# Attention's product with V by tiles of 128 queries, and GpSimd's first row requests placed behind the first mixed low parts

## The reference, cut to what matters

```
for i in range(2):
    y = rms_norm(h, mix_norm[i]);  proj = y @ w_in[i]
    mixed = concatenate([lru_out * silu(g_lru), ret_out * silu(g_ret), sgu_out * silu(g_sgu)])   # 2048 wide
    h = h + mixed @ w_out[i]
    z = rms_norm(h, ple_norm[i]);  h = h + sigmoid(z @ w_ple_gate[i]) * (p[i] @ w_ple_proj[i])
```

```
mod = silu(cond) @ w_ada + b_ada                       # shifts, scales and gates, 6 x 1024
s = einsum('bqkgd,bskd->bkgqs', q, k) * 128 ** -0.5    # 4 query heads, 2 key heads, 512 queries, 768 keys
o = einsum('bkgqs,bskd->bqkgd', softmax(s), v)
x = x + gt1 * (concatenate([o, conv], -1) @ w_out)
x = x + gt2 * moe_ffn(modulate(x, ...))                # 32 experts, 4 per token
```

## Time and profile before

| | |
|---|---|
| time, median of 3 runs | 2527.57 us (2526.86 to 2530.43) |
| the profiled execution's own time | 2525.92 us |
| its span | 2524.1 us |
| PE busy | 2420.9 us, 96% of the span |
| DVE, ACT, POOL busy | 2036.4, 1319.5, 683.3 us |
| mean granted TensorE clock | 0.977 of full speed |

### The profile page before, as it was taken

How to read it: one execution, slowest core, us unless ns; L and a number is a source line. 1 busy time by engine, 2 the same in 40 slices (tenths; PEclk the granted TensorE clock), 3 DMA queues, 4 the chain that set the end, 5 groups by cost and what they waited for, 6 DMA issues and landing times.

```text
span 2524.1 us, 31372 instructions
## 1 busy us (share of the span) xinstructions
PE 2420.9 (96%) x10771; PEld 1934.3 (77%) x10771; DVE 2036.4 (81%) x1844; ACT 1319.5 (52%) x1206; POOL 683.3 (27%) x407
## 2 busy tenths in 40 slices
PE   8999999999999999998869999999999999999995
PEld 7777778786877787874657888888888888888884
DVE  7788587576885786884259999999999999999994
ACT  4442223334323244334327777777777777777772
POOL 5333341342423432340221222122112211221120
PEclk9999999999999999999969999999999999999998
DMA  6232245222422652220049999999999999999992
GB/s 236 83 130 71 75 152 174 67 76 78 139 67 82 257 211 69 75 93 1 13 177 372 367 373 366 378 365 372 368 371 370 373 361 380 361 372 368 375 358 96
DMA packets 104426, 572.47 MB, mean 227 GB/s; under 512 B 14192, under 2 KB 14336, under 8 KB 54288
## 3 DMA queue, kind: packets, MB, share of 16 engines
q1 hardware_dynamic: 86784, 515.15, 53.9%
q0 software_dynamic: 17280, 56.20, 7.7%
q10 hardware_dynamic: 288, 0.14, 0.0%
HBM read 559.37 MB, written 24.12 MB: 231 GB/s over the span
## 4 chain that ended last, share of the span: by engine, by line
PE 89%; DVE 6%; ACT 2%; issue 1%; DVEq 1%; DMA 1%; ACTq 0%; SPq 0%; POOLq 0%
PE ps L1479 85%; PE ps L1157 2%; DVE scr L2180 1%; DVE y_split L2117 1%; PE ps L665 0%; DVE mix L2231 0%; DVE scr L2229 0%; DMA mix<-acc_rows 0%; DVE scr L948 0%; DVEq L2127 0%; PE ps L701 0%; DMA acc_rows<-rows,lst 0%; DVE w_split L1284 0%; PE ps L1409 0%; DVE hT L2377 0%
## 5 line engine op out<-in xcount | busy, mean ns | idle before, releaser
L1284 DVE TENSOR_TENSOR w_split<-raw,w_split 128x2048 fp32r<-128x2048 f32 x386 | 877.3, 2287 | 54.6 <-ACT w_split L1236 43.5
L1479 PE MATMUL ps<-y_split,pieces_split 128*128 128x512 f32 x3600 | 846.9, 396 | 19.6 <-POOLq L2547 7.8
L1236 ACT ACTIVATE w_split<-raw 128x2048 fp32r<-128x2048 f32 x386 | 736.1, 1916 | 197.8 <-PE ps L1479 178.2
L1479 PEld LDWEIGHTS ps<-y_split,pieces_split 128*128 128x128 f32 x3600 | 681.9, 190 | 172.4 <-issue 29.0
L1479 PE MATMUL ps<-w_split,rows_T 128*128 128x512 f32 x3096 | 752.2, 394 | 1.9 <-DVE rows_T L1290 1.9
L1479 PEld LDWEIGHTS ps<-w_split,rows_T 128*128 128x128 f32 x3096 | 575.5, 188 | 119.4 <-DVE rows_T L1290 2.5
L2535 POOL TENSOR_TENSOR pieces_split<-pieces,pieces_split 128x1024 fp32r<-128x1024 f32 x151 | 373.2, 2482 | 653.5 <-ACT pieces_split L1813 524.9
L1813 ACT ACTIVATE pieces_split<-pieces 128x1024 fp32r<-128x1024 f32 x144 | 151.3, 1058 | 434.5 <-PE ps L1479 403.2
L1479 PE MATMUL ps<-w_split,hidden_T 128*128 128x512 f32 x1536 | 363.7, 392 | 1.7 <-DVE hidden_T L1290 1.7
L1479 PEld LDWEIGHTS ps<-w_split,hidden_T 128*128 128x128 f32 x1536 | 285.8, 188 | 72.5 <-DVE hidden_T L1290 13.5
L1348 POOL COPY rows_i<-slot_tokens 128x1 int32 (+1 forms) x34 | 59.5, 1750 | 407.7 <-PE ps L1157 374.0
(11 more groups left out here) (265 smaller groups left out, 2074.9 us busy)
## 6 DMA issues: line engine op xcount, KB each, us to landing
raw<-in_w_moe SPq DMA_DIRECT2D x386, 1024.0 KB, 7.5
pieces<-in_pieces SPq DMA_DIRECT2D x181, 512.0 KB, 3.6
scr<-in_ada POOLq DMA_DIRECT2D x48, 512.0 KB, 5.4
scr<-in_ple SPq DMA_DIRECT2D x2, 1536.0 KB, 7.0
acc_rows<-in_zeros POOLq DMA_DIRECT2D x5, 512.0 KB, 10.9
hT<-in_xT SPq DMA_DIRECT2D x8, 256.0 KB, 5.5
h_rows<-scr SPq DMA_DIRECT2D x4, 512.0 KB, 3.5
mix<-acc_rows SPq DMA_DIRECT2D x4, 512.0 KB, 5.1
```

The lines of the kernel that those rows point to most:

```text
L1236: nc.scalar.activation(wsp[:, p % SPLIT, 0], raw[:, p % RAW, :], ACT.Copy).then_inc(high, 3 if p == 1 else 1)
L1284: nc.vector.tensor_tensor(wsp[:, p % SPLIT, 1], raw[:, p % RAW, :], wsp[:, p % SPLIT, 0].bitcast(F32), ALU.subtract).then_inc(low, 3 if p ...
L1479: return pe.matmul(out, lhsT, rhs, start=start, stop=stop)
```

## The change

In attention, the product with V is done for each tile of 128 queries, one turn behind its probabilities, into banks 6 and 7 in turn (`o_tile`), and DVE copies each tile out two turns behind. The scores have two places instead of three, since the third held banks 6 and 7. All counts of `o_ready` become counts of tiles.

In the two layers, `mixed_low` of tiles 0 to 4 (with the low part of `wo.4` between) is placed ahead of POOL's first requests for rows of `w_ada`.

```diff
-        SCORE_BANK = (0, 2, 6)
+        SCORE_BANK = (0, 2)
+        def o_tile(n):
+            return ps[:, 6 + n % 2, 0:P]
...
-                h, t, b = n // ST, n % ST, SCORE_BANK[n % 3]
-                if n >= 3:
-                    pe.wait_ge(exp_ready, n - 2)
+                h, t, b = n // ST, n % ST, SCORE_BANK[n % 2]
+                if n >= 2:
+                    pe.wait_ge(exp_ready, n - 1)
...
                 for j in range(KT):
-                    if j == 4 and n % ST == 0 and n:
-                        pe.wait_ge(o_ready, n // ST)
                     m = pe.transpose(...)
+            def attended(n):
+                h, t = n // ST, n % ST
+                pe.wait_ge(pt_ready, n + 1)
+                if n >= 2:
+                    pe.wait_ge(o_ready, n - 1)
+                for j in range(KT):
+                    m = mm(o_tile(n), vall[:, j, (h // 2) * P:(h // 2 + 1) * P], eT[:, j, t * P:(t + 1) * P],
+                           j == 0, j == KT - 1)
+                m.then_inc(o_full, 1)
...
                 turned(n)
-                if n % ST == ST - 1:
-                    h = n // ST
-                    pe.wait_ge(pt_ready, n + 1)
-                    for j in range(KT):
-                        m = mm(ps[:, 5, :], vall[...], eT[:, j, :], j == 0, j == KT - 1)
-                    m.then_inc(o_full, 1)
-            pe.wait_ge(o_ready, QH)
+                if n >= 1:
+                    attended(n - 1)
+            attended(QH * ST - 1)
+            pe.wait_ge(o_ready, QH * ST)
...
+            def o_out(n):
+                h, t = n // ST, n % ST
+                dve.wait_ge(o_full, n + 1)
+                nc.vector.tensor_copy(mix[:, 8 + h, t * P:(t + 1) * P], o_tile(n)).then_inc(o_ready, 1)
...
-                if n % ST == ST - 1:
-                    h = n // ST
-                    dve.wait_ge(o_full, h + 1)
-                    nc.vector.tensor_copy(mix[:, 8 + h, :], ps[:, 5, :]).then_inc(o_ready, 1)
+                if n >= 2:
+                    o_out(n - 2)
+            o_out(QH * ST - 2)
+            o_out(QH * ST - 1)
...
-                    if k == 0:
+                    for tile in range(4) if k == 0 else [4] if k == 1 else []:
+                        mixed_low(layer * 16 + tile + 1, tile % DK, tile)
+                    if k == 1:
                         pool.wait_ge(V.full, V.done(layer, "o5"))
                         for i in range(ADA_RAW[layer]):
                             ada_load(i)
-                    for tile in range(4) if k == 0 else [4] if k == 1 else []:
-                        mixed_low(layer * 16 + tile + 1, tile % DK, tile)
```

More of the change, by code:

```diff
@@ L674, in tail_pe @@
                 turned(n)
-                if n % ST == ST - 1:
-                    h = n // ST
-                    pe.wait_ge(pt_ready, n + 1)
-                    for j in range(KT):
-                        m = mm(ps[:, 5, :], vall[:, j, (h // 2) * P:(h // 2 + 1) * P], eT[:, j, :], j == 0, j == KT - 1)
-                    m.then_inc(o_full, 1)
-            pe.wait_ge(o_ready, QH)
+                if n >= 1:
+                    attended(n - 1)
+            attended(QH * ST - 1)
+            pe.wait_ge(o_ready, QH * ST)
             pe.wait_ge(conv_ready, 4)
@@ L814, in tail_act @@
                     act.wait_ge(pt_full, n - 1)
-                b, c = SCORE_BANK[n % 3], 16 + n % 3
+                b, c = SCORE_BANK[n % 2], 16 + n % 3
                 s_ = ps[:, b:b + 2, :].rearrange("p a b -> p (a b)")[:, 0:KEYS]
@@ L824, in tail_act @@
                 if n > ST and n % ST == 2:
-                    act.wait_ge(o_ready, n // ST)
+                    act.wait_ge(o_ready, n // ST * ST)
                     mixed_high(n // ST - 1)
             turned_copy(act, QH * ST - 1)
-            act.wait_ge(o_ready, QH)
+            act.wait_ge(o_ready, QH * ST)
             mixed_high(QH - 1)
```

## The result

| | before | after |
|---|---|---|
| time, median | 2527.57 us (4 runs, 2526.86 to 2530.43) | 2508.31 us (4 runs, 2506.66 to 2509.06) |
| ratio to before, 95% interval | | 0.9918 [0.9904, 0.9932] |
| the profiled execution's own time, span | 2525.92, 2524.1 us | 2509.06, 2507.2 us |

The predicted 2508 us is 0.3 us from the median. The changed kernel was timed again on two other occasions: 2510.16 us (ratio 0.9924 [0.9911, 0.9938]) and 2510.17 us (0.9926 [0.9912, 0.9939]).

What follows compares the result with a forecast made beforehand. PE was taken to bound the kernel, with 89% of the chain of waits. Attention's 10.6 us plus the output projections' 9.2 us took 19.8 us off 2525.92, 2508 us as a median; range 2503 to 2511, chance 0.62.

Steps and rivals of the forecast that it cites:

- PE works alone in each head's block, and a lag removes that: Attention: the product with V one tile behind covers PE's waits of 0.3 to 0.9 us a turn; gain 10.6 us.
- A record of 128 columns costs 0.117 us also when it accumulates: Attention: a tile's 12 records take 1.40 us as in the gating, making a turn 3.44 us of PE.
- rivals 2 and 3: Attention: weight loads or accumulation pace short products, 2522 us, chance 0.07; or accumulating records take 0.28 us each, 2540, 0.05.
- DVE and ACT fit under PE's turn: Attention: both engines' work per turn, 3.1 us for DVE, stays below PE's 3.44 us.
- rival 4: Attention: DVE or ACT stays last, a turn of 4.1 us leaves no gain there; 2518 us, chance 0.08.
- The third place for scores costs nothing: Attention: two places for scores cost nothing; only the third scores wait about a microsecond, where PE stands anyway.
- The shorter gap keeps the clock: Output projection's start, both layers: a 1.4 us gap keeps full clock; gain 3.8 + 5.4 = 9.2 us.
- The delay of the requests costs nothing: Output projection: POOL's later requests still bring rows in time, with 4.4 us to spare at tile 5 in the second layer.
- An idle stretch of over a microsecond in the second layer's projection: Second layer's output projection: such an idle stretch of PE was named as showing the forecast wrong.
- Rival 1: Output projection: clock still falls, or late rows make PE wait at tile 5 or 6; 2512 to 2515 us, chance 0.18.
- The sum: Whole kernel: 10.6 us from attention and 9.2 us from the output projections, 19.8 us off, giving 2508 us.

Runs made afterwards that it cites:

- experiment 5: Changed kernel without the one turn's lag of the product with V, done in the same turn as its probabilities: 2529.47 us, ratio 1.0006.
- Experiments 6 and 7: Changed kernel with 1 and 2 (then 2 and 3) first requests in the two layers ahead of the first mixed low part, rest behind: 2512.48 and 2515.33 us.
- experiment 9: The changed kernel timed again, nothing edited: 2510.17 us.
- experiment 4: Changed kernel with POOL's first requests for rows right behind the first mixed low part instead of the fifth: 2508.68 us, ratio 0.9916.
- 8: Changed kernel with requests right behind the first mixed low part and the context's 1 MB transfer four pieces later in the second layer: 2506.92 us, ratio 0.9919.
- experiment 10: Changed kernel with only the context's 1 MB transfer four pieces later in the second layer: 2508.50 us, ratio 0.9922.

## Why the prediction was right, and the step of it that failed

- **PE works alone in each head's block, and a lag removes that.** Right. From the third turn to the thirteenth PE doesn't wait, and experiment 5 shows that without the lag the gain is gone.
- **A record of 128 columns costs 0.117 us also when it accumulates.** Right in kind, a little high. The last 24 records take 2.84 us with their end, the last 12 take 1.50: (2.84 - 1.50) / 12 = 0.112 us. A turn is 3.28 us, not 3.44, the transposes 0.65, not 0.71. Eleven full turns at 0.15 to 0.16 us less are 1.7 us of the 2.2 us between 10.6 and the measured 12.75; the rest is in the last tiles. Against the figures of the Trainium skill ("TensorE: Matmul & The Clock Gate", section Back-to-back issue gap) the measurement decides: four short products take no longer than one long, where its figures would have them 2.5 times as long. With that rivals 2 and 3 fall.
- **DVE and ACT fit under PE's turn.** Right; rival 4 falls. One turn near the end waits for DVE, 0.25 us.
- **The third place for scores costs nothing.** Right but for the one wait foreseen, 1.02 us at the third scores.
- **The shorter gap keeps the clock.** Right, 1.30 us each (1.4 predicted), gains of 3.5 and 5.2 us for 3.8 and 5.4. Experiments 6 and 7 show both terms and that the clock's share goes here once the gap is 2.4 us. The reason given for the longer of the two low parts, DVE at work beside it, is not in the rows: DVE is busy beside both, 6.49 of 6.61 us and 5.40 of 5.40.
- **The delay of the requests costs nothing.** This step failed, by about 2.4 us in the profiled execution and up to 4.7 us more in that of experiment 9. Its numbers for tile 5 were right (low part at 849.56, and 852.7 predicted with the second layer still standing 3.2 us later; 3.6 us to spare, 4.4 predicted). The failure is in "From then on DVE's turns are 48.1 / 9 = 5.34 us, PE's 5.44, so the margin doesn't shrink". Those rows begin at tile 6. The turn from tile 5 to tile 6, with rows 5 to 7, took 857.33 - 849.56 = 7.77 us, 1.8 of them waiting for rows, and left PE's tile 6 only about 1.3 us to spare. From there DVE kept its pace and never made the 2.4 us good. PE still had its tiles in time, and there the prediction's sums ended: I followed the delay to PE's next tiles and stopped. DVE's last own low part has a second customer, POOL's low parts of the gate's pieces, and there the kernel before had only a microsecond to spare: they ended at 912.19 + 9.05 = 921.24, and PE needed them at about 922.3 (8.4 us after 904.71 + 9.23 = 913.94, where the changed kernel's PE is done with what it has). From there PE came 8.4 us earlier, DVE 5.95. An idle stretch of over a microsecond in the second layer's projection was one of the prediction's own signs of being wrong; 1.76 us came right behind its last tile. Rival 1 had late rows in it, but at PE's tile 5 or 6, where PE has no wait. With the requests early, DVE's waits for rows 5 to 7 go once the context's transfer stands elsewhere (4.96 us in experiment 4, 0.34 in 8); with the requests late, moving the transfer brought nothing in sum (experiment 10).
- **The sum.** The 2.2 us too few in attention and the 2.4 us not foreseen in the requests nearly cancel. That the median came within 0.3 us of 2508 is partly luck; each term alone was off by more.

What is open: why the clock falls sooner or later in the one-column products, and how much of an earlier start there is kept. PE is never idle in them. In experiments 4 and 8 they started 1.7 and 3.0 us earlier, the clock fell at 935 and 934 us instead of 938, came back at 949 and 948 (948 in the changed kernel), and 1.7 and 1.6 us of the lead were lost. No run here was made to tell whether that is a rule.

## What to carry to other kernels

Split a product only as far as needed to run it one step behind its inputs; the split alone can cost more than it brings, and the lag is what covers the copy between two engines. When an issue of DMAs is moved behind work on the same engine, follow its data to the last consumer, not to the next one: compare how much earlier the fast engine arrives at each meeting point with how much earlier the delayed chain does, and look for the meeting with the least to spare in the profile of before. A wait ahead of the bounding engine can cost about its own length again in clock (2.70 us of waiting and 2.86 us of slower products in experiment 9). At the start of the projection that was gone when the gap was down from 3.2 to 1.9 us, and at 2.4 us not yet; in the routing a gap of 2.4 us kept the clock in eight executions of eleven.

## What the runs showed that I had not expected

- 128-column products that accumulate over six steps in one place go by at 0.112 us a record, the same per column as 512-column ones.
- The granted clock behind a gap of TensorE at the start of the projection: 1.00 for gaps of 1.30 and 1.89 us, 0.54 to 0.60 for 2.40, 2.43 and 3.21 us. In the routing 2.38 us left it at 1.00 in one execution and at 0.58 in another.
- The same wait in the same kernel was 1.74, 1.76 and 2.70 us in three executions, as the first row landed sooner or later. Only the last one brought the clock down, to 0.50, and attention then started 4.7 us later; in the 3.07 us of experiment 10 the clock fell too, and attention started 0.4 us later.
- In 64 one-column products the clock fell with TensorE never idle, from 938 us in the changed kernel, and from 934 or 935 us where they started earlier.
